# Three attention loops rolled into hardware loops, and three state transfers sent unpacked

## The reference, cut to what matters

```python
# attention over the prompt, per head
s = jnp.where(key_pos[None, :] <= qpos[:, None], s, -jnp.inf)
p = jax.nn.softmax(s, axis=-1).astype(ckv.dtype)
return jnp.einsum('bhqs,bsk->bqhk', p, ckv)

# pooling mixer: prev is the saved state, 15 rows for each sequence
xp = jnp.concatenate([prev.astype(h.dtype), h], axis=1)
...
return jnp.concatenate(outs, axis=-1) * ls, xp[:, -POOL_BUF:]

# convolution: prev is the saved state, 2 rows for each sequence
up = jnp.concatenate([prev.astype(u.dtype), u], axis=1)
...
return y, up[:, -CONV_BUF:]
```

## Time and profile before

| | |
|---|---|
| Time before, median of 3 | 2707.22 us |
| The profiled execution's own time | 2707.22 us |
| Its span, first to last instruction | 2705.1 us |
| TensorE busy | 2512.9 us (93%) |
| VectorE busy | 1697.0 us (63%) |
| ScalarE busy | 1276.2 us (47%) |
| GpSimd busy | 321.5 us (12%) |
| Mean granted TensorE clock | 0.974 |
| HBM traffic | 244.88 MB read, 7.07 MB written |

### The profile page before, as it was taken

How to read it: one execution, slowest core, us unless ns; L and a number is a source line. 1 busy time by engine, 2 the same in 40 slices (tenths; PEclk the granted TensorE clock), 3 DMA queues, 4 the chain that set the end, 5 groups by cost and what they waited for, 6 DMA issues and landing times.

```text
span 2705.1 us, 48959 instructions
## 1 busy us (share of the span) xinstructions
PE 2512.9 (93%) x18858; PEld 2286.5 (85%) x18858; DVE 1697.0 (63%) x3281; ACT 1276.2 (47%) x2926; POOL 321.5 (12%) x349
## 2 busy tenths in 40 slices
PE   6786999999979889999999999999999999999995
PEld 2775666666657888999999999999989999999995
DVE  3513555555622357776667885876885877776665
ACT  4322343343411566544446655555554555544443
POOL 0000000000000243000003211302312301200003
PEclk9897999999989989999999999999999999999998
DMA  5102222222364412222222222223222222232221
GB/s 216 43 17 84 90 90 90 90 90 79 115 218 139 177 56 85 79 93 88 87 87 102 79 86 71 79 86 109 99 71 79 87 81 92 87 122 86 93 87 63
DMA packets 70982, 255.10 MB, mean 94 GB/s; under 512 B 7746, under 2 KB 15298, under 8 KB 64354
## 3 DMA queue, kind: packets, MB, share of 16 engines
q1 hardware_dynamic: 70034, 251.27, 26.3%
q10 hardware_dynamic: 720, 0.71, 0.1%
HBM read 244.88 MB, written 7.07 MB: 93 GB/s over the span
## 4 chain that ended last, share of the span: by engine, by line
PE 50%; DVE 10%; ACT 3%; issue 3%; POOL 1%; DMA 0%; POOLq 0%; ACTq 0%; DVEq 0%
PE psum L2461 10%; PE psum L2460 10%; PE psum L2459 10%; PE psum L2434 5%; PE psum L2436 5%; PE psum L2435 5%; DVE t_conv L2295 3%; DVE t_w_lo L2277 2%; DVE t_y L2327 1%; PE psum L2416 1%; PE psum L2418 1%; PE psum L2000 1%; PE psum L2417 1%; DVE t_scaled L1772 1%; POOL t_stat L1926 1%
## 5 line engine op out<-in xcount | busy, mean ns | idle before, releaser
L2459 PE MATMUL psum<-t_h,t_w_hi 128*128 128x272 f32 x2816 | 817.0, 290 | 3.2 <-DVE t_w_lo L2277 3.2
L2461 PE MATMUL psum<-t_h,t_w_lo 128*128 128x272 f32 x2816 | 813.5, 289 | 0.0
L2460 PE MATMUL psum<-t_h,t_w_hi 128*128 128x272 f32 x2816 | 812.4, 288 | 0.0
L2459 PEld LDWEIGHTS psum<-t_h,t_w_hi 128*128 128x128 f32 x2816 | 531.8, 189 | 4.5 <-DVE t_w_lo L2277 3.4
L2460 PEld LDWEIGHTS psum<-t_h,t_w_hi 128*128 128x128 f32 x2816 | 532.1, 189 | 1.1
L2461 PEld LDWEIGHTS psum<-t_h,t_w_lo 128*128 128x128 f32 x2816 | 532.0, 189 | 0.0
L2434 PE MATMUL psum<-t_g_hi,t_w_hi 128*128 128x272 f32 x1408 | 411.2, 292 | 27.8 <-DVE t_w_lo L2277 16.6
L2295 DVE SCALAR_TENSOR_TENSOR t_conv<-t_u,t_taps,t_conv 128x272 f32<-128x272 f32 (+2 forms) x528 | 339.1, 642 | 151.8 <-ACT t_conv L2199 145.6
L2327 DVE TENSOR_TENSOR t_y<-psum,t_y 128x272 f32<-128x272 f32 x640 | 279.5, 437 | 202.6 <-PE psum L2436 198.3
L2435 PE MATMUL psum<-t_g_lo,t_w_hi 128*128 128x272 f32 x1408 | 406.1, 288 | 0.0
L2436 PE MATMUL psum<-t_g_hi,t_w_lo 128*128 128x272 f32 x1408 | 405.5, 288 | 0.0
(11 more groups left out here) (213 smaller groups left out, 3619.6 us busy)
## 6 DMA issues: line engine op xcount, KB each, us to landing
t_raw<-in_ffn_w SPq DMA_DIRECT2D x264, 512.0 KB, 3.5
late_w<-in_ada_late SPq DMA_DIRECT2D x40, 1024.0 KB, 4.8
cache<-in_cache SPq DMA_DIRECT2D x64, 320.0 KB, 4.9
ada_w<-in_ada_w SPq DMA_DIRECT2D x4, 2048.0 KB, 19.5
t_raw<-in_wo SPq DMA_DIRECT2D x16, 512.0 KB, 3.8
pair_raw<-in_pair_w SPq DMA_DIRECT2D x8, 768.0 KB, 6.3
x<-in_x SPq DMA_DIRECT2D x2, 2176.0 KB, 10.7
out_x_out<-x SPq DMA_DIRECT2D x4, 1088.0 KB, 5.9
```

Source lines behind the costliest of these rows:

```text
L2459: pe.matmul(bank, t.w_hi[s][:, o], hi, start=kt == 0, stop=False)
L2460: pe.matmul(bank, t.w_hi[s][:, o], lo, start=False, stop=False)
L2461: last = pe.matmul(bank, t.w_lo[s][:, o], hi, start=False, stop=kt == KT - 1)
```

## The change

In prompt attention the loop over j becomes a hardware loop on each of the three engines (`act.Fori`, `dve.Fori`, `pe.Fori`). j is then a register, and values and addresses that depend on it are worked out by register instructions.

In the tail the packed copies go. The pooling state is loaded straight into `room.hs`, where each sequence has 15 saved rows and 8 new ones, in runs of 15 numbers (60 bytes), and is counted on the semaphore of the pool's weights. It is stored straight from `room.tail` and `room.hs` by two transfers of such runs, one unit earlier. The three copies on ScalarE go with their semaphores. The convolution's state is loaded without its two zeros, in runs of 16 numbers (64 bytes).

```diff
@@ ScalarE; the same on VectorE (dve.Fori) and TensorE (pe.Fori)
-            for j in range(HP // 2 - 1):
+            with act.Fori(0, HP // 2 - 1) as j:
                 pair(2 * j + 1, 1, 16 * j + 32, j, 1)
                 pair(2 * j + 2, 0, 16 * j + 32, j, 2)
@@ Chain.act
-                    act.wait_ge(t.pool_out, 16)
+                    act.wait_ge(t.pool_out, 32)
...
             if kind == "pool":
-                act.wait_ge(t.past_put, 1)
+                act.wait_ge(t.pool_w_in, 48)
                 dst = self.room.hs[:, :, :, BUF:]
...
-        if self.plan.windows and self.half and tick == PAST_PUT:
-            act.wait_ge(t.past_in, 16)
-            act.activation(self.room.hs[:, :, :, 0:BUF], self.room.past, ACT.Copy).then_inc(t.past_put, 1)
-        if self.plan.windows and self.half and tick == KEPT_PUT:
-            act.wait_ge(t.window_f, self.after["window_f"])
-            act.wait_ge(t.put_s, self.at["entry_s"] + 1)
-            act.activation(self.room.kept[:, :, 1:, :], self.room.hs[:, :, :, DEC_S:], ACT.Copy)
-            act.activation(self.room.kept[:, :, 0, :], self.room.tail, ACT.Copy).then_inc(t.kept_put, 1)
@@ Chain.pool_window
-            if self.half:
-                pool.wait_ge(t.past_put, 1)
@@ Chain.pe
-            pe.wait_ge(t.pool_w_in, 16 * (self.half + 1))
+            pe.wait_ge(t.pool_w_in, 48 if self.half else 16)
@@ SyncE in the tail
             def conv_state(layer):
-                sp.dma_start(t.state[:], io["conv_state"][:, layer]).then_inc(t.state_in, 16)
+                sp.dma_start(t.state[:, :, 0:16], io["conv_state"][:, layer, :, 0:16]).then_inc(t.state_in, 16)
...
                 if chain.half:
-                    sp.dma_start(chain.room.past, io["pool_state"]).then_inc(t.past_in, 16)
+                    sp.dma_start(chain.room.hs[:, :, :, 0:BUF], io["pool_state"]).then_inc(t.pool_w_in, 16)
 
             def give_pool(chain):
-                sp.wait_ge(t.kept_put, 1)
-                sp.dma_start(io["pool_out"], chain.room.kept).then_inc(t.pool_out, 16)
+                sp.wait_ge(t.put, 2 * KT * (chain.at["entry"] + 1))
+                sp.wait_ge(t.put_s, chain.at["entry_s"] + 1)
+                sp.dma_start(io["pool_out"][:, :, 0, :], chain.room.tail).then_inc(t.pool_out, 16)
+                sp.dma_start(io["pool_out"][:, :, 1:, :], chain.room.hs[:, :, :, DEC_S:]).then_inc(t.pool_out, 16)
...
-                if n == 2 * PAIRS + 12:
+                if n == 2 * PAIRS + 11:
                     give_pool(chains[3])
```

More of the change, by code:

```diff
@@ L946, in _ @@
             pair(0, 0, -1, 2, first=True)
-            for j in range(HP // 2 - 1):
+            with dve.Fori(0, HP // 2 - 1) as j:
                 pair(2 * j + 1, 1, j, 1)
@@ L1082, in _ @@
             pair(0, 0, -1, 2, first=True)
-            for j in range(HP // 2 - 1):
+            with pe.Fori(0, HP // 2 - 1) as j:
                 pair(2 * j + 1, 1, j, 1)
@@ L1404 @@
 WINDOWS_BY_POOL = [[(0, 48, 51), (1, 52, 57)], [(0, 48, 50), (1, 51, 53)]]
-PAST_PUT, KEPT_PUT = 40, 70
 SAMPLE_WINDOWS = [(0, 55, 56), (1, 57, 58), (2, 59, 61), (3, 62, 64)]
@@ L1458, in __init__ @@
         self.pool_w_in, self.pool_out = sem("pool_w_in"), sem("pool_out")
-        self.past_in, self.past_put, self.kept_put = sem("past_in"), sem("past_put"), sem("kept_put")
         self.pool_done, self.pool_evac = sem("pool_done"), sem("pool_evac")
@@ L1507, in __init__ @@
             at += n
-            packed = room[:, 2 * GT * self.span:2 * GT * self.span + KT * N_SEQ * BUF]
-            self.past = packed[:, 0:KT * DEC_B * BUF].rearrange("p (k s n) -> p k s n", k=KT, s=DEC_B)
-            self.kept = packed.rearrange("p (k s n) -> p k s n", k=KT, s=N_SEQ)
             self.tail = room[:, at:at + KT * BUF].rearrange("p (k n) -> p k n", k=KT)
@@ L2133, in _ @@
             sp.wait_ge(t.state_out, 32)
-            sp.wait_ge(t.pool_out, 16)
+            sp.wait_ge(t.pool_out, 32)
             sp.wait_ge(t.x_out, 64)
```

## The result

| | before | after |
|---|---|---|
| Median | 2707.14 us (2706.04 to 2712.79, 4 runs) | 2743.45 us (2741.11 to 2746.53, 4 runs) |
| Profiled execution, its span | 2707.22, 2705.1 us | 2748.43, 2746.6 us |
| Mean granted TensorE clock | 0.974 | 0.964 |

After is slower by 1.34%: the ratio is 1.0134, 95% interval 1.0120 to 1.0147. The forecast was 2720.0, slower. The sign is right, and the time lies inside the range of 2704 to 2752, but the change costs 36 us where 13 were forecast. The profiled execution is 5 us slower than the median of its kernel. TensorE had lost 2.6 us against before when pair 1 began, and lost 2.6 more between the start of pair 7 and the store. This part is left out of the account.

The account below looks back on a forecast made before the run. The prediction took TensorE to set the pace, so that additions cost time only where it waits. It added 8.5 us for the loops and 4.3 for the state's transfers to 2707.2, giving 2720.0 us, range 2704 to 2752.

Parts of the forecast that it names:

- the store: Tail, pooling state's store issued one unit earlier: 576 runs an engine, 14.4 us of transfer, no stall; 10.5 at 51 ns.
- The branches: Prompt attention's loops: one entry and two returns on three engines at 1.63 us each, 4.9 us together.
- the register instructions: Prompt attention, pairs 1 to 6: 0.05 us each, 0.6 us a pair at six waiting places, 3.6 us; upper end 25.
- the 4.3 us at the pooling state's load: Tail: 12.8 us of transfer against a limit of 8.5 before TensorE waits for U's weights, a stall of 4.3 us.
- What bounds the kernel: Prompt attention and tail run at TensorE's pace, busy 93% of the span; additions cost only if TensorE waits.
- a return costs over 3 us: Prompt attention's loops: a stated sign that the forecast is wrong; gaps of one to two us were expected at returns.
- Price of a run: Tail's state transfers: 25 ns for each short run on a DMA engine, between ends of 18 and 51 ns.
- Convolution's state: Tail, its load: 352 runs an engine, 8.8 us against a limit of 12.0, so no stall; 6.0 us at 51 ns.
- the limit of 18.9: Tail's store: the transfer time in us up to which TensorE would not wait for U's weights, needed at 2082.2 us.
- ScalarE's copies: Tail: removing three copies, 2.35 us of ScalarE, gains nothing, since TensorE has no gap there.
- The second: Rival: tail's scattered transfers are dear, 51 ns a run, 17.6 + 6.0 + 10.5 = 34 us, 2750 with part 1 (loops); chance 0.14.
- The third: Rival: loops are dear, register rows on every step's chain, 25 + 4.9 = 30 us, 2741 with part 2 (transfers); chance 0.11.

Follow-up runs that it names:

- e7: Kernel before with only the change's two unpacked loads (pooling state and convolution's state), loops and store as before: 2711.89 us, ratio 0.9993.
- e10: Kernel before with only the unpacked store, cut into nine pieces of 1024 runs of 60 bytes, one behind each weight load: 2712.74 us, ratio 1.0001.
- e12: Changed kernel with VectorE's loop written out, TensorE's and ScalarE's returns announced, store in nine pieces: 2711.67 us, ratio 1.0001 to the kernel before.
- e3: Kernel before with the hardware loop on TensorE alone, VectorE and ScalarE written out: 2724.03 us, ratio 1.0056.
- e5: Kernel before with the three hardware loops, each return announced at the head of a round: 2721.47 us, ratio 1.0050.
- e9: Kernel before with only the unpacked store, its 60-byte runs each beginning on a multiple of 64 bytes: 2714.96 us, ratio 1.0007.
- e8: Kernel before with only the unpacked store, output rows padded so runs write 64 bytes on multiples of 64: 2714.67 us, ratio 1.0003.

## Why the prediction was right or wrong

The forecast added 12.8 us and 36.3 were measured. Its largest failed step is the store, put at nothing: it costs 16.6 us. The branches (4.9 for 11.3) and the register instructions (3.6 for 8.5) were too small, and the 4.3 us at the pooling state's load did not occur. That the time lies inside the stated range says little for the sum: no term that was given a price came out at that price.

- **What bounds the kernel: right.** TensorE's pace sets both places, and every microsecond lost is one in which it waits or has a lower clock.
- **Branches, 4.9 us: failed; they measure 11.3.** The upper end was taken from a branch forward at a stage's start, 1.63 us. A return goes back to instructions that have gone by. The entry cost nothing, the two returns 5.6 each. The forecast named "a return costs over 3 us" as what would make it wrong, and it did. No row of before bounded the fetch, but the trace of before had the other half of its price: the DMA engines are busy for 0.26 of a pair, and the last of these transfers are issued at its very end (`late_w` from 431.43 us on and `pair_raw` at 441.62, pair 3 beginning at 443.06). The Trainium skill (Runtime: NRT & Kernel Launch, Instruction fetch mechanics) says that a taken branch outside the held window must wait for a fetch, and I left it at a sentence. With that rule the trace agrees for TensorE, whose round has 2057 instructions in the trace (1105 rows and 952 matmuls) against the page's 2048, and for ScalarE, whose 253 return in 0.3 us. VectorE's 348 are under the 512 that the page gives an engine and wait all the same; the page's other figure, two pages of 256 read in sequence, can fit them. That is a fit and no test, since no run varies the length of a round.
- **Register instructions, 3.6 us: too small; 8.5.** The direct delay is 0.24 us in a pair at the late step, less than the 0.6 taken. The price is what the longer wait does to the granted clock: 1.4 to 1.7 us of slower matmuls behind it, at one place and not at six, and in four of the six pairs. The rule applied, delay times places, has no term for the clock. The reading of the places was a little off too: the earlier trace rows gives 1.7 us for L1057's three waits, the longest 1.2, so that the other two are 0.5 together and not 0.4 or more each.
- **Price of a run, 25 ns for every transfer: wrong in both directions.** A load's run costs 12.7 ns, under the lower end of 18. A store's costs 46 in one long store, near the upper end of 51, and 13 when it fills an aligned piece of 64 bytes. One price for loads and stores was the mistake. That the earlier trace rows, a store, gave a figure near 46 is luck: its packets have 1088 bytes, and what makes these runs dear is how they lie on the 64-byte pieces.
- **Pooling state, a stall of 4.3 us: none.** 6.5 us of transfer against a limit of 8.5; the limit's reasoning was not tested.
- **Convolution's state, nothing: right.**
- **The store, nothing: 16.6.** Price and limit both failed. With 46 ns and the limit of 18.9, X = 26.8 gives 7.9. The limit measures 11.8, since the first work that is late is not TensorE's use of U's weights (2082.2 us in before) but ScalarE's rounding of them (2073.15), behind which `t_y` stands in order. The earlier trace rows shows only G's last evacuation; ScalarE's own order between two of them was to be read.
- **ScalarE's copies, nothing: right** (`e7`, `e10`, `e12`).
- **Rivals.** The second came nearest at the store (10.5 us of 16.6) and was wrong on both loads. The third was too high for the loops (30 us against 20) and from a mechanism that did not occur: the register chain of each step. Forecast and rivals had one price for all runs and one for all engines' branches; ScalarE's loop and the loads turned out free.

## What to carry to other kernels

A hardware loop with a long round (here 2057 instructions on TensorE and 348 on VectorE, but not 253 on ScalarE) pays for each return with a fetch through the same DMA engines as the data: announce the return, or keep large transfers away from it. Price short runs by direction, by the 64-byte pieces they cover and by how many stand in a row, loads and stores apart, and put many of them behind one another only where the next block has room. That room ends where the first in-order engine wants the block, whatever it is for, and a short delay in front of TensorE is to be priced with its clock.

## What the runs showed of the hardware

- A return of TensorE's loop lost 5.6 us beside 1.7 MB of transfers (5.7 in `e3`) and 2.8 with the DMA engines quiet (2.61 idle). Announced a round ahead, its branch took under 0.5 and nothing was lost (`e5`).
- A wait of 1.25 us instead of 1.01 was followed, in four of the six pairs of after, by a granted clock of 0.65 instead of 1.00 over the next 40 matmuls (3.5 us became 4.9); in the other two the clock stayed at 1.00.
- Short writes to HBM in one long store: 13 ns for 64 bytes on a multiple of 64, 26 for 60 bytes there, 46 for 60 bytes at a pitch of 60, the first 2 us of each at 10 to 12. In pieces of 1024 runs at a pitch of 60, 15 to 23. Loads of 60-byte runs packed at 60 bytes in HBM: 12.7. The Trainium skill (DMA: Bandwidth & Descriptors, Specifications) puts read-modify-write at transfers under 512 bytes; here size alone does not decide, since 64 bytes in place cost as little as a load's run.
- SyncE itself stops when it issues behind such a store: the issue of one weight block took 14.7 us in after, 5.1 with aligned runs of 60 bytes (`e9`), and 0.33 where the runs fill their 64-byte pieces (`e8`).
